# Attention scores of two heads as two 64-row products into banks 0 and 1, in a fused two-block forward pass

## The reference

```python
# hybrid layer: 8 heads of 64, dense after the three dilated patterns are merged into one mask
s = jnp.einsum("bhrnqd,bhrnkd->bhrnqk", qs, kb) * (1.0 / math.sqrt(D))
s = jnp.where(valid, s, NEG_INF)
m = jnp.max(s, axis=-1)
p = jnp.exp(s - m[..., None])
l = jnp.sum(p, axis=-1)
o = jnp.einsum("bhrnqk,bhrnkd->bhrnqd", p, vb) / l[..., None]
# sparse mixer: 16 heads of 64 in 4 groups; selected blocks (ss) and window (sw), both causal
ss = jnp.einsum('bghtd,bgtnld->bghtnl', qb, kg).astype(jnp.float32) * ATTN_SCALE
sw = jnp.einsum('bghtd,bkgd->bghtk', qb, kwb).astype(jnp.float32) * ATTN_SCALE
```

## Time and profile before

| | |
|---|---|
| median of three runs | 2093.42 (2089.79 to 2094.72) |
| the profiled execution's own time | 2096.46 |
| its span | 2094.4 |
| PE / DVE / ACT busy | 95% / 57% / 46% of the span |
| chain that ended last | PE 82%, DVE 10%, ACT 5%; L556 57%, L2822 10%, L932 1%, L995 1% |
| data moved | 524.40 MB, mean 250 GB/s, expert weights from about 1188 on |

### The profile page before, as it was taken

One profiled execution on the slowest core, in us unless ns is written; L12 is line 12 of the kernel. 1 busy time (PEld: TensorE's weight loads), 2 busy tenths in 40 slices (PEclk: granted clock), 3 DMA queues, 4 the chain that ended last, 5 costly groups with the idle time before them and its releaser, 6 DMA issues.

```text
span 2094.4 us, 27829 instructions
## 1 busy us (share of the span) xinstructions
PE 1996.8 (95%) x10836; PEld 1481.1 (71%) x10836; DVE 1203.7 (57%) x1356; ACT 969.9 (46%) x1140; POOL 20.9 (1%) x33
## 2 busy tenths in 40 slices
PE   8889999988999999999998899999999999999997
PEld 7767998776799878887776566766666566656653
DVE  4875545597554564457666755454554555445454
ACT  5554444555444444444454444443444444444444
POOL 0000000000000000000000000000000000000000
PEclk9999999998999999999879999999999999999999
DMA  7413555441465535553300299999999999999995
GB/s 286 144 48 116 201 188 194 142 145 47 153 217 188 196 130 184 199 181 139 108 22 1 113 370 409 417 418 409 387 411 411 393 382 412 412 395 376 422 420 230
DMA packets 74665, 524.40 MB, mean 250 GB/s; under 512 B 8768, under 2 KB 9216, under 8 KB 12192
## 3 DMA queue, kind: packets, MB, share of 16 engines
q1 hardware_dynamic: 71712, 511.64, 62.5%
q0 software_dynamic: 2816, 10.93, 1.5%
HBM read 521.48 MB, written 1.05 MB: 249 GB/s over the span
## 4 chain that ended last, share of the span: by engine, by line
PE 82%; DVE 10%; ACT 5%; issue 3%; DMA 1%; SPq 0%; DVEq 0%; ACTq 0%
PE psum L556 57%; PE psum L2822 10%; PE psum L2873 5%; DVE AR L1733 2%; PE psum L932 1%; PE psum L995 1%; PE psum L2940 1%; ACT HI L539 1%; DVE LO L2771 1%; PE psum L756 1%; PE psum L2125 1%; PE psum L2834 1%; PE psum L737 1%; ACT HI L2764 1%; PE psum L2962 1%
## 5 line engine op out<-in xcount | busy, mean ns | idle before, releaser
L556 PE MATMUL psum<-HI,XT 128*128 128x512 f32 (+1 forms) x2080 | 533.3, 399 | 25.3 <-ACT HI L2764 6.4
L547 DVE TENSOR_TENSOR LO<-ring,HI 128x2048 fp32r<-128x2048 f32 (+1 forms) x157 | 346.8, 2214 | 280.8 <-ACT HI L539 280.8
L556 PEld LDWEIGHTS psum<-HI,XT 128*128 128x128 f32 x2080 | 391.1, 194 | 148.8 <-issue 37.9
L539 ACT ACTIVATE HI<-ring 128x2048 fp32r<-128x2048 f32 (+1 forms) x157 | 289.7, 1849 | 230.5 <-PE psum L556 229.7
L556 PE MATMUL psum<-LO,XT 128*128 128x512 f32 (+1 forms) x1040 | 281.8, 394 | 1.5 <-DVE LO L2771 1.1
L2771 DVE TENSOR_TENSOR LO<-ring,HI 128x2048 fp32r<-128x2048 f32 x84 | 191.1, 2288 | 86.5 <-ACT HI L2764 80.9
L556 PEld LDWEIGHTS psum<-LO,XT 128*128 128x128 f32 x1040 | 198.4, 193 | 45.5 <-DVE LO L2771 4.7
L556 PE MATMUL psum<-HI,HTH 128*128 128x512 f32 x568 | 228.2, 402 | 0.0
L556 PE MATMUL psum<-HI,HTL 128*128 128x512 f32 x568 | 222.3, 391 | 0.0
L2764 ACT ACTIVATE HI<-ring 128x2048 fp32r<-128x2048 f32 x84 | 159.4, 1910 | 84.9 <-DMA ring<-in_experts 73.7
L2771 DVE TENSOR_TENSOR LO<-AR,HI 128x2048 fp32r<-128x2048 f32 x64 | 145.8, 2288 | 67.7 <-ACT HI L2764 67.5
(11 more groups left out here) (329 smaller groups left out, 2177.4 us busy)
## 6 DMA issues: line engine op xcount, KB each, us to landing
ring<-in_experts SPq DMA_DIRECT2D x172, 1024.0 KB, 9.2
ring<-in_dense SPq DMA_DIRECT2D x149, 1024.0 KB, 4.9
AR<-in_experts SPq DMA_DIRECT2D x84, 1024.0 KB, 9.7
cons<-in_experts SPq DMA_DIRECT2D x42, 1024.0 KB, 9.2
bcs<-in_experts SPq DMA_DIRECT2D x38, 1024.0 KB, 8.5
bcs<-in_ln_g POOLq DMA_DIRECT2D x4, 512.0 KB, 6.4
bcs<-in_ln_b POOLq DMA_DIRECT2D x4, 512.0 KB, 5.4
bcs<-in_norm_g POOLq DMA_DIRECT2D x3, 512.0 KB, 3.9
```

The source lines that it names most:

```text
L539: e.activation(HI[:, h:h + m], slot(u), ACT.Copy).then_inc(*high.up(u))
L547: e.tensor_tensor(LO[:, h:h + m], slot(u), HI[:, h:h + m].bitcast(F32), ALU.subtract).then_inc(*(freed if u in early else low).up(u))
L556: ins = e.matmul(out_ap, lhsT=a, rhs=b, start=start and n == 0, stop=stop and n == len(pairs) - 1)
```

## The change

The scores of a tile become two products. Head h uses partitions 64h to 64h + 63 of the queries and of its own block of `kz`, and writes bank h; both banks are held for every tile. The mask reads the same columns of banks 0 and 1 in one operation and waits for both products. The turn of tile n goes to bank 2 + n % 2. So these no longer move the counter of `take`, and what comes after them in the program gets other banks than before; in the last attention the counter is set to 0 before the first output transposes.

```diff
         def att_weigh(e, a, n):
             kind, qt, b = a.todo[n]
             nk = att_keys(a, n)
-            bank = banks.take(e, a.name, "s", n)
+            for h in range(2):
+                banks.hold(e, h, a.name, "s", n)
             for w in a.ready(kind):
                 e.wait_ge(*w)
-            e.matmul(bank[:, 0:2 * nk], lhsT=a.qT[:, b, tile(qt)], rhs=a.kz(kind, b)[:, :, 0:nk],
-                     start=True, stop=True).then_inc(*filled.up(a.name, "s", n))
+            for h in range(2):
+                rows_ = slice(h * 64, h * 64 + 64)
+                ins = e.matmul(psum[:, h, 0:nk], lhsT=a.qT[rows_, b, tile(qt)],
+                               rhs=a.kz(kind, b)[rows_, h, 0:nk], start=True, stop=True)
+                ins.then_inc(*filled.up(a.name, "s", n, *([] if h else [0])))
...
         def att_mask(e, a, n):
...
+            e.wait_ge(*filled.of(a.name, "s", n, 0))
             e.wait_ge(*filled.of(a.name, "s", n))
...
             e.scalar_tensor_tensor(
-                w3, banks.get(a.name, "s", n)[:, 0:2 * nk].rearrange("p (h k) -> p h k", h=2), 0.125,
+                w3, psum[:, 0:2, 0:nk], 0.125,
                 bc3(a.mask[:, qt, 0:nk], 2, 1), ALU.mult, ALU.add).then_inc(*v_bank.up(a.name, "s", n))
...
         def att_turn(e, a, n):
             kt = att_keys(a, n) // P
-            bank = banks.take(e, a.name, "t", n)
+            bank = banks.hold(e, 2 + n % 2, a.name, "t", n)
...
             def y_tile(t):
+                if t == 0:
+                    banks.n = 0
```

## The result

The changed kernel takes 2143.07 us (median of four runs, 2139.66 to 2148.66); the kernel before, run beside it, 2091.70 (2089.79 to 2094.72). The ratio is 1.024, with a 95% interval of 1.0222 to 1.0258: slower by about 50 us. The forecast of 2110.2 had the direction and a third of the size, and the time lies 22 us outside the range of 2096 to 2121. The profiled execution took 2143.82 us with a span of 2142.0 (2094.4 before).

The account below looks back on a forecast made before the run. The prediction saw PE busy 95% of the span, but no engine full in attention, where waits count. Eight steps of lost run-ahead sum to 16.8 us, on the median 2093.42 giving 2110.2; range 2096 to 2121.

Parts of the forecast that it names:

- The price of a pair: Score products: two 64-row products run side by side, 0.63 us for 256 keys, about 0.42 for 128.
- The layers: Fillers and mLSTM turns on score banks wait for masks: +2.8 us in layer 0 (1.4 to 3.5), +2.9 in layer 1.
- start, mask(3): Sparse attention, start: scores(2) wait for mask(1), so the second half of the key compression runs later: +2.5 us (2.0 to 3.0).
- scores(6), mask(7): Sparse attention: scores(6) wait for mask(5), and the work up to mask(7) hangs on them: +1.15 us (0 to 3.5).
- scores(8), mask(9): Sparse attention: scores(8) wait for mask(7), with a half compression behind them: +3.15 us at mask(9) (1.0 to 4.2).
- yc(1) with mask(26): Later sparse attention: scores(24) wait for tc(1), turn(22) for yc(1,1)'s bank, scores(26) behind: +2.2 us for both (1.1 to 2.6).
- The clock: Rival, 6%: new gaps lower PE's clock; ten more us of PE work at half clock give 2120 to 2126.
- the saved PE time being inside each step: In the sum: the lighter pairs' 10 to 11 us of saved PE time were already counted within the steps.
- the two signs of being wrong: Forecast wrong if the attention stretches grow by less than 8 us in sum, or L935's records don't overlap.
- the waits hide: Rival, 9%: masks nearly always end within the turns and gather, and the pair pays: between 5 and 11 us less, say 2084.
- lateness is absorbed: Rival, 10%: late scores only fill slack of DVE and ACT, gains and losses cancel: 2089 to 2098.
- the halves do not overlap: Rival, 3%: a pair costs about 1.06 us, 0.43 more for some 20 scores on the path: 2119.

Follow-up runs that it names:

- the run-ahead kept: The pair in the two layers alone, in banks that let PE's scores run a tile ahead, sparse part as before: 2095.12 us, ratio 1.0009.
- layers-only kernel: The change in the two layers with 8 tiles alone, the sparse part as in the kernel before: 2099.24 us, ratio 1.0028.
- sparse-only kernel: The change in the sparse part alone, the layers as in the kernel before: 2136.66 us, ratio 1.0209.
- waits filled: The change plus 12 products of nobody's use where PE would wait for the mask in the sparse part: 2117.41 us, ratio 1.0120.
- waits alone: The change with one full-width score product instead of the pair, its waits for the mask kept: 2133.20 us, ratio 1.0189.
- the pair without them: The change with scores of even tiles in banks 0 and 1, odd in 2 and 3, turns in gather banks: 2123.20 us, ratio 1.0134.
- the control: One full-width score product instead of the pair, even and odd tiles' scores in separate banks, turns in gather banks: 2108.79 us, ratio 1.0070.

## Why the prediction was right and wrong

**The price of a pair: right.** 0.63 was forecast for 256 keys and 0.64 measured (522.11 to 522.75). For 128 keys it is 0.42 (1132.39 to 1132.81), as forecast. The halves overlap. That it would win nothing by itself in the layers was not said so plainly: with the run-ahead kept, the time is that of before.

**The layers: right in cause and in the sum, with some luck in the sum.** Forecast 2.8 + 2.9 = 5.7; measured 6.7 by the first mask and the next weight product, 5.7 by the layers-only kernel, and the cause was isolated. Of the 6.7, layer 0 has 4.9, above its high bound of 3.5, and layer 1 has 1.8. That split is uncertain: the sparse-only kernel, whose layers are those of before, has 29.1 and 26.0 where the kernel before has 26.2 and 28.8, in sum the same. In layer 0 the filler of step 7 waited for the mask of tile 7:

```profile
155.52 0.69 DVE L954 SCALAR_TENSOR_TENSOR AR<-psum,cons 128x512 f32<-128x512 f32 x1
...
156.27 1.12 PE L737 MATMUL psum<-cons 128*128 128x512 f32 x2 [1.81 <-DVE AR L954]
...
158.56 0.51 ACT L966 ACTIVATE AR<-AR,SML 128x256 f32<-128x256 f32 x1
```

exp(7) came at 158.56 instead of 153.52: 5.0, of which 3.45 were there at mask(7), from the start of this attention. There 1.4 was forecast, and L1831 moved by 3.2 (144.82 against 141.58), because filler and mLSTM gather ran at half clock (2.08 and 1.56). Layer 1 gave 2.4 for 2.9 by its stretch.

**The sparse part: the places right, the sizes wrong.** By the shift of masks against before:

| step of the forecast | forecast | measured | waits filled |
|---|---|---|---|
| start, mask(3) | 2.5 | 2.4 | 2.7 |
| scores(6), mask(7) | 1.15 | 3.9 | 1.3 |
| scores(8), mask(9) | 3.15 | 5.9 | 3.1 |
| compressed scores, mask(13) | 0.6 | 3.6 | 1.4 |
| tiles 14 to 16 | 0 | 4.3 | 0.3 |
| tc(0) and yc(0), masks 17 to 19 | 1.5 | 6.4 | 2.8 |
| masks 20 to 24 | 0 | 3.1 | 2.0 |
| yc(1) with mask(26) | 2.2 | 3.4 | 1.5 |
| masks 27 to 31, output transposes | 0 | 7.8 | 0.1 |

(The 2.2 had the wait for tc(1) in it, which is in masks 20 to 24 here. The measured column adds up to 40.8 from mask(0), which was itself 2.0 less late than the first scores, hence 38.8 for the stretch.) The wait of L2344 was to grow to over 5, and was 7.3 in two. At the second of them, DVE's timeline of the changed kernel:

```profile
1084.19 0.16 DVE L2344 COPY SML<-psum 128x1 f32<-128x1 f32 x1 [3.75 <-PE psum L2130]
```

The half compression in front of it took 5.1 us for 3.3 (1078.83 to 1083.97), at half clock to its end. With the waits filled the whole column is 15.2 instead of 40.8, and the forecast for it was 11.1: the steps are largely those forecast, but in the change most of what stands behind a wait ran at 1.2 GHz.

**The step that failed** is the last rival, "The clock": "Ten more us of PE work at half clock give 2120 to 2126", at 6%. The trace had shown how much of this part hung on the clock, 0.82 in rows 1, and a product costs twice as much at half clock in rows 2 and 6. I took the drop as one event with a fixed price and kept the terms at the clock that each stretch had before. Only the high bounds of two of them had it, 3.5 at mask(7) and 4.2 at mask(9), and both were passed (3.9 and 5.9). It is a loop instead: a wait lowers the clock, the work behind it takes longer, and the lighter tile then leaves PE at half clock even when it has work all the time (tiles 13 to 15). It cost 27.5 us of longer PE time. By the filled waits, which give 26 us back with every dependency in place, what is left of the change is 2117, 7 over the forecast and inside the range. The rule cited from the Trainium skill (TensorE: Matmul & The Clock Gate, HAM oscillation), that gaps bring the half clock back, was the better guide, although its example is of longer waits, for DMA, and the longest here for the mask was 3.2 us: the trace agrees, with 0.71 for waits alone. The gaps were not all of it, as the pair without them ran at 0.59.

The step before it failed too, in sign: "the saved PE time being inside each step" took the lighter product as a gain at worst lost. It is a loss of 9 to 12 us in this stretch where nothing fills the gap it leaves. And one sum is off: the high bounds, with the extra wait, add up to 25.2 and not 24, which moves the upper end by 1 us. Neither of the two signs of being wrong asked whether the stretches grow by far more than forecast, which is what happened.

The rivals by which the waits hide, lateness is absorbed or the halves do not overlap are refuted by the same rows. No version here beats the kernel before: the nearest, with pairs and a run-ahead in the layers alone, is equal to it.

Open: why the kernel before held 0.81 with waits of its own, how much of the control's 15 us lies in the turns' new banks, and whether anything in the 64-row products besides their fewer columns bears on the clock. None was tried.

## What to carry to other kernels

When a change makes PE's work lighter or makes it wait, write the sum twice, once with everything behind each wait at half clock, and let the range reach the second. Before giving up a buffer for a faster product, ask who else takes those banks: fillers and small transposes that moved onto them were the whole loss in the layers. A cheap test of a clock theory is a useless product put exactly where the engine would wait; if the kernel gets faster by it, the dependencies were not all that cost.

## What the runs showed that I had not expected

Less work can take longer: a tile with the pair took 3.80 us at half clock with no wait in it, the heavier tile of before 2.19 at full clock. More work can take less: with a filler of 0.97 us in it such a tile took 2.97, and twelve fillers took 26 us off the kernel. And a raised clock alone earns nothing: fillers took the kernel before from 0.81 to 0.86 in the sparse stretch and made it 3 us longer.
